# Two experts of a mixture-of-experts kernel are fixed in the first two whole units, and two shared units move in among the routed ones

## The reference

```python
def moe_ffn(h, router_w, router_bias, w_gu, w_down, shared_gu, shared_down):
    scores = jax.nn.sigmoid(jnp.dot(h, router_w, ...))
    _, idx = lax.top_k(scores + router_bias, TOP_K)          # TOP_K = 6 of 64 experts
    gates = jnp.take_along_axis(scores, idx, axis=-1)
    gates = gates / jnp.sum(gates, axis=-1, keepdims=True) * ROUTED_SCALE
    ...                                                      # no capacity limit, no dropped tokens
        y = swiglu(h_pad[src_b], w_gu[e], w_down[e])         # 1024 -> 2x384 -> 1024
        return y * gate_b[:, None]
    ...
    return routed + swiglu(h, shared_gu, shared_down)
```

## Time and profile before

| | us |
|---|---|
| median of 3 runs | 3029.93 (3028.95 to 3030.8) |
| the profiled execution, device time | 3032.81 |
| its span | 3030.9 |
| PE busy | 2432.6 (80%) |
| DVE / ACT / POOL busy | 800.4 / 425.1 / 316.4 |
| DMA moved | 776.00 MB, of which HBM read 770.98 MB |
| mean granted PE clock | 0.904 of full speed |

### The profile page before, as it was taken

The page is one execution under the profiler, slowest core; times in us unless marked ns, Lnnn a source line. Parts: engine busy times, 40 slices in busy tenths (PEclk is TensorE's granted clock), DMA queues, the critical chain, the costliest instruction groups (busy, mean ns, idle before and its releaser), DMA issues. The chain is left out here.

```text
span 3030.9 us, 36674 instructions
## 1 busy us (share of the span) xinstructions
PE 2432.6 (80%) x15133; PEld 1334.9 (44%) x15133; DVE 800.4 (26%) x1601; ACT 425.1 (14%) x854; POOL 316.4 (10%) x374
## 2 busy tenths in 40 slices
PE   5978869999899888988870797929877888888882
PEld 2447625555444444444430356816543434444331
DVE  2214564324211111111015413574421111111112
ACT  1022323310000000000000203215100000000000
POOL 0015200000011111110100004300001111101000
PEclk8989978799999999999995898959989999999996
DMA  7010266333899999999956110001489999999992
GB/s 266 24 51 3 71 224 224 128 123 124 327 426 424 416 400 402 390 402 406 398 213 256 47 46 2 3 9 67 183 347 428 421 419 421 413 413 416 410 393 108
DMA packets 122428, 776.00 MB, mean 256 GB/s; under 512 B 34648, under 2 KB 45032, under 8 KB 65808
## 3 DMA queue, kind: packets, MB, share of 16 engines
q1 hardware_dynamic: 99216, 735.75, 60.1%
q0 software_dynamic: 23040, 37.82, 3.3%
HBM read 770.98 MB, written 44.44 MB: 269 GB/s over the span
## 5 line engine op out<-in xcount | busy, mean ns | idle before, releaser
L1330 PE MATMUL banks<-arena,htreg 128*64 128x384 f32 (+1 forms) x4288 | 905.5, 515 | 129.3 <-DMA arena<-in_exp_w_gu 119.5
L1330 PEld LDWEIGHTS banks<-arena,htreg 128*64 128x64 f32 (+1 forms) x4288 | 448.0, 155 | 594.9 <-issue 366.8
L1350 PE MATMUL banks<-arena,modreg 128*64 128x512 f32 (+1 forms) x1608 | 439.9, 607 | 74.2 <-DMA arena<-in_exp_w_down 32.5
L1941 DVE TENSOR_TENSOR modreg<-modreg,banks 128x384 f32<-128x384 f32 x80 | 44.3, 554 | 967.2 <-ACT modreg L1564 967.2
L1350 PEld LDWEIGHTS banks<-arena,modreg 128*64 128x64 f32 (+1 forms) x1608 | 165.4, 150 | 294.9 <-issue 294.9
L2244 POOL DMA_INDIRECT y_d<-modreg,lst x74 | 73.6, 994 | 1362.8 <-DVE modreg L2081 1346.5
L953 PE MATMUL banks<-arena,htreg 128*128 128x428 f32 x512 | 184.2, 522 | 0.0
L1564 ACT ACTIVATE modreg<-banks 128x384 f32<-128x384 f32 x80 | 39.2, 490 | 998.0 <-PE banks L1330 998.0
L2081 DVE COPY modreg<-banks 128x512 f32<-128x512 f32 x74 | 51.2, 692 | 437.0 <-PE banks L1350 437.0
L953 PEld LDWEIGHTS banks<-arena,htreg 128*128 128x128 f32 x512 | 97.3, 190 | 86.9 <-issue 86.9
L1576 ACT ACTIVATE modreg<-banks 128x512 f32<-128x512 f32 x74 | 44.2, 597 | 440.0 <-PE banks L1350 440.0
(11 more groups left out here) (377 smaller groups left out, 2298.0 us busy)
## 6 DMA issues: line engine op xcount, KB each, us to landing
arena<-in_exp_w_gu SPq DMA_DIRECT2D x256, 1536.0 KB
arena<-in_exp_w_down SPq DMA_DIRECT2D x128, 1536.0 KB
modreg<-in_w_mod SPq DMA_DIRECT2D x40, 1024.0 KB, 5.0
arena<-y_d SPq DMA_DIRECT2D x6, 3072.0 KB, 17.6
arena<-in_w_in SPq DMA_DIRECT2D x8, 1712.0 KB, 10.8
modreg<-mod_d SPq DMA_DIRECT2D x20, 512.0 KB, 6.3
arena<-in_w_out SPq DMA_DIRECT2D x2, 4096.0 KB, 13.6
arena<-in_w_mod SPq DMA_DIRECT2D x6, 1024.0 KB, 9.3
```

Of the source, the lines that this page charges most:

```text
L1330: last = mm(ps[2 + half][rows, 0:DE], src[:, k, rows], up4[q][:, i, DE * half:DE * (half + 1)], start=(k == 0), stop=(k == KD - 1))
L1350: last = mm(ps[4 + half][rows, :], actT[:, k, rows], dn3[q][:, k, 512 * half:512 * half + 512], start=(k == 0), stop=(k == KE - 1))
```

## The change

Experts 0 and 1 get sort keys above all others, and so ranks 0 and 1, whatever their numbers of rows. SP loads their weights by constant index before it waits for the sort. The order of units becomes: two shared ones, then whole unit 0, the third shared, whole unit 1, the fourth shared (layer 1 has only two shared ones), then the rest, with whole units somewhat denser and the last four or five paired ones alone at the end. A chunk goes to the slot that comes free first. The shared units behind the first two get their transposed input in the way of a routed unit. On PE both list steps stand before `unit_down(1)`; on DVE the lists come before `unit_times(1)`, and the addresses of the general lists and `maxcnt` come behind the first `unit_copied`. `WHOLE`, `UNITS`, `cap` and the branch on `maxcnt` stay.

```diff
 WHOLE = (16, 4)
+GIVEN = 2
...
+        EARLY = 2
...
-            order = []
+            order = [whole.pop(0) for _ in range(GIVEN)]
+            early = len(paired) - 4
             for i in range(len(paired)):
                 order.append(paired[i])
-                while whole and (len(order) - i) * len(paired) <= (i + 1) * WHOLE[l]:
+                while whole and (len(order) - i - 1) * early < (i + 1) * WHOLE[l]:
                     order.append(whole.pop(0))
             return order + whole
...
+        def with_shared(l):
+
+            routed = work(l)
+            order = [(None, (i,)) for i in range(EARLY)]
+            for i in range(EARLY, NOUT[l]):
+                order += [routed.pop(0), (None, (i,))]
+            return order + routed
...
+        freed = lambda l, c: (c[0] or LAST_SHARED[l], PARTS.index(c[1]))
+
+        def ring(l):
+
+            slot_of, held = {}, {}
+            for i, c in enumerate(CHUNKS[l]):
+                q = i if i < SLOTS else min(held, key=lambda q: freed(l, held[q]))
+                slot_of[c], held[q] = q, c
+            return slot_of
...
                 sp.wait_ge(lists_cleared.sem, lists_cleared.at(l, 1))
-                sp.wait_ge(sorted_ready.sem, sorted_ready.at(l, 1))
...
+                    if r0_sorted(n):
+                        sp.wait_ge(sorted_ready.sem, sorted_ready.at(l, 1))
+                    experts = [r if r < GIVEN else sp.value_load(eid[0:1, r:r + 1], min_val=0, max_val=NE - 1) for r in ranks]
...
-                unit_up(1)
-                lists_by_expert()
+                unit_up(1, between=lists_by_expert if n_t == 2 else None)
+                if n_t > 2:
+                    lists_by_expert()
+                lists_by_unit()
                 unit_down(1)
-                lists_by_unit()
-                for n in range(2, NSH[l]):
-                    unit_up(n)
-                    unit_down(n)
-                unit_transposed(NSH[l])
-                for n in range(NSH[l], NW[l]):
+                unit_transposed(EARLY)
+                for n in range(EARLY, NW[l]):
                     unit_up(n)
                     if n + 1 < NW[l]:
                         unit_transposed(n + 1)
                     unit_down(n)
...
                 link(stt(key, cnt, float(NE), K("experts"), ALU.mult, ALU.subtract))
+                link(ts(key[:, 0:GIVEN], K("experts")[:, 0:GIVEN], -1.0, float(NO_CODE), ALU.mult, ALU.add))
...
-                unit_times(1)
                 dve.wait_ge(slot_hot_used.sem, slot_hot_used.at(l, TOPK * n_t))
                 dve.tensor_copy(listT, ps[1][lo64, 0:P]).then_inc(listT_ready.sem, 1)
-                shared_out(1)
...
+                unit_times(1)
+                shared_out(1)
...
+                unit_copied(EARLY)
+                overflow_addresses()
+                for n in range(EARLY, NW[l]):
...
-                pool.wait_ge(gu_psum.sem, gu_psum.at(l, NSH[l]))
+                pool.wait_ge(gu_psum.sem, gu_psum.at(l, EARLY))
```

More of the change, by code:

```diff
@@ L802, in load_expert, with one_of @@
                                  ).then_inc(X["w"][b].sem, 16)
+                def one_of(e):
+                    return slice(e, e + 1) if isinstance(e, int) else bass.ds(e, 1)
                 def load_chunk(c, experts):
@@ L826, in _ @@
                             if loaded >= SLOTS:
-                                m, was, _ = CHUNKS[l][loaded - SLOTS]
-                                m = max(m, NSH[l] - 1)
-                                sp.wait_ge(free_by[was].sem, free_by[was].at(l, m + 1))
+                                q = SLOT_OF[l][n, part, j]
+                                was = in_slot(l, q)[SEQ_OF[l][n, part, j] - 1]
+                                by = free_by[was[1]]
+                                sp.wait_ge(by.sem, by.at(l, freed(l, was)[0] + 1))
                             if loaded == SLOTS - 1:
@@ L1305, in unit_transposed @@
                 def unit_transposed(n):
[L1306 to L1309, removed]
+                    q = n - EARLY
+                    if is_shared(l, n):
+                        src = h[:, OUT_TILES[l][WORK[l][n][1][0]], :].rearrange("p (k d) -> p k d", k=KD)
+                    else:
+                        r = ROUTED_AT[l].index(n)
+                        pe.wait_ge(gathered[r % 2].sem, gathered[r % 2].at(l, r // 2 + 1))
+                        src = slots[r % 2].rearrange("p (d k) -> p k d", k=KD)
+                    if q:
+                        pe.wait_ge(slotT.sem, slotT.at(l, q))
                     for k in range(KD):
-                        last = pe.transpose(ps[k // 4][:, tok(k % 4)], slots[r % 2].rearrange("p (d k) -> p k d", k=KD)[:, k, :], ident)
+                        last = pe.transpose(ps[k // 4][:, tok(k % 4)], src[:, k, :], ident)
                     last.then_inc(slotT_psum.sem, 1)
                 def unit_up(n, between=None):
-                    if n >= NSH[l]:
-                        pe.wait_ge(slotT.sem, slotT.at(l, n - NSH[l] + 1))
-                        src = hgT[(n - NSH[l]) % 2]
+                    if n >= EARLY:
+                        pe.wait_ge(slotT.sem, slotT.at(l, n - EARLY + 1))
+                        src = hgT[(n - EARLY) % 2]
                     else:
@@ L2032, in _ @@
                          ALU.mult, ALU.mult))
[L2033 to L2049, removed]
+                def overflow_addresses():
+                    link(ts(base, rank, float(U_), float(HALF * U_ - U_ + W_), ALU.is_ge, ALU.mult))
+                    link(tt(base, base, rank, ALU.add))
+                    link(tt(cnt, cnt, cap, ALU.subtract))
+                    link(red(cntmax[:, 0:1], cnt, AX, ALU.max))
+                    link(ts(cntmax[:, 1:2], cntmax[:, 0:1], float(P), None, ALU.add))
+                    link(dve.tensor_copy(maxcnt[0:1, 0:1], cntmax[0:1, 1:2]))
+                    link(stt(adr[:, nt_, :], pos[:, nt_, :], float(U_), bc(base, 1, n_t), ALU.mult, ALU.add))
+                    link(stt(adr2[:, nt_, :], pos[:, nt_, :], float(NE), bc(K("experts"), 1, n_t), ALU.mult, ALU.add))
+                    link(stt(adr2[:, nt_, :], adr2[:, nt_, :], float(LIST1), adr[:, nt_, :], ALU.add, ALU.subtract))
+                    link(tt(adr2[:, nt_, :], adr2[:, nt_, :], over[:, nt_, :], ALU.mult))
+                    link(tt(adr[:, nt_, :], adr[:, nt_, :], adr2[:, nt_, :], ALU.add))
+                    for i in range(n_t):
+                        link(tt(ohp, onehot[:, i], bc(adr[:, i, :], 1, TOPK), ALU.mult))
+                        link(red(posk[:, i, 0:TOPK], ohp, AX, ALU.add))
+                    dve.tensor_copy(addr[:, nt_, 0:TOPK], posk[:, nt_, 0:TOPK]).then_inc(addr_ready.sem, 1)
@@ L2066, in unit_copied @@
                 def unit_copied(n):
[L2067 to L2073, removed]
+                    q = n - EARLY
+                    dve.wait_ge(slotT_psum.sem, slotT_psum.at(l, q + 1))
+                    dve.tensor_copy(hgT[q % 2][:, 0:4, :], ps[0][:].rearrange("p (k n) -> p k n", k=4))
+                    dve.tensor_copy(hgT[q % 2][:, 4:8, :], ps[1][:].rearrange("p (k n) -> p k n", k=4)).then_inc(slotT.sem, 1)
+                unit_copied(EARLY)
+                overflow_addresses()
+                for n in range(EARLY, NW[l]):
                     unit_times(n)
```

57 lines of the change are left out of this document (31 added, 26 removed).

## The result

| | before | after |
|---|---|---|
| median us | 3029.44 (3025.36 to 3030.8) | 12095.69 (12059.91 to 12145.55) |
| ratio | | 3.9937, 95% interval 3.9819 to 4.0055 |
| span of the profiled execution | 3030.9 | 12065.1 |
| mean granted PE clock | 0.904 | 0.808 |

The change makes the kernel four times as long. The forecast was 12,450 us, with 11,190 to 14,260 as its range. The four runs of the changed kernel lie 86 us apart, so a kernel with the loop that ran once is read to some tens of microseconds.

What follows compares the result with a forecast made beforehand. Both layers were taken as bound by streaming expert weights, PE close behind in layer 0. The sum was 3032.8 - 33 + 9470 = 12,470, less 2.9 to the runs' median, 12,467, said as 12,450 us; range 11,190 to 14,260.

Steps and rivals of the forecast that it cites:

- The branch: After layer 0's units: a 65-row expert at rank 16 exceeds cap 64, so 256 loop steps run; none in layer 1.
- The step of the loop: Layer 0's loop: load and matmuls follow one another, 37.0 us a step (32 to 44), 9470 us for 256 steps.
- load, issue to first matmul: Start of each loop step: 4608 KB of weights, scaled from w_out's landing, take 15.3 us.
- gathered rows in place: Loop step, beside the load: copy, scatter, gather and transposes take 10.0 to 19.9 us, about 13, hidden behind the load.
- gate and up: Loop step's first matmuls on PE: 10.48 us plus 2.9 for the low clock, 13.4 us (10.5 to 16).
- down: Loop step's down projection on PE: 5.39 us, up to 7.09 when the clock fell.
- the branch back: End of each loop pass over four steps: possible instruction fetch of 2.8 us, 180 us in all, making the time 12,650.
- rival 3: The gather sets the loop step's front, landing at 12.7 us: step 41.6 us, time 13,650; chance 8 in 100.
- The rest of the change: Everything outside the loop: early weights, layer 1's start, both layer ends and the moved list chain together give -33 us.
- By then 14 or 15 chunks are requested, as many as before at 815.: Layer 0's start: four units end near 811 with weight requests level with before; gain 3 us.
- PE follows the last landing by one down and little more, 7 us instead of 25.: Layer ends: with pairs last, PE finishes sooner after the last weights; gain 18 us in each layer.
- layer 1's start: Layer 1: two whole units first draw too few weight chunks, partly offset by lists 5.4 us sooner; net loss of 6.

Runs made afterwards that it cites:

- one_round: Changed kernel with R = [1, 1], so the loop makes one round of 64 experts instead of four; 5300.8 us (one run).
- key_only: Kernel before plus only the line giving experts 0 and 1 ranks 0 and 1; 12,091 us (one run), with 256 loop loads.
- fixed_1_15: Changed kernel with experts 1 and 15, the fullest of layer 0, fixed instead of 0 and 1; no loop, 3029.2 us, ratio 0.9992 to before.
- before_pairs_last: Kernel before with whole units mixed a little denser, so four or more paired units stand last in each layer; 3017.8 us, ratio 0.9954.
- fixed_late: fixed_1_15 with SP's wait for the sort put back ahead of the first expert's load; ratio 0.9995.
- fixed_even: fixed_1_15 with the old mixing of the other whole units, so a whole one stands last in both layers; 3044.9 us, ratio 1.0044.

## Why the prediction was right, and where it was off

**The branch.** Right as told. One row of expert 37 was over, layer 0 took the loop for it, layer 1 did not. The argument used counts only; no busy time of before could have shown it.

**The step of the loop.** Forecast 37.0 us, measured 35.3, inside the 32 to 44 taken. By terms:

| term | forecast | in the step shown | mean of all steps |
|---|---|---|---|
| load, issue to first matmul | 15.3 | 14.1 | 14.4 (with the last row) |
| gathered rows in place | 13, hidden | 13.4, hidden by 0.7 | |
| gate and up | 13.4 | 12.0 | 12.5 |
| silu to copy | 2.4 | 2.4 | 2.4 |
| down | 5.4 | 5.4 | 6.0 |
| branch, semaphores | 0.5 | 0.2 | |

The means are worked out from the page's lines of L1296, L1306, L1314 and L1320 above, busy and idle time over 256; they add up to 35.4. Two terms were too large: the front by 1.4 us (15.3 + 0.5 against 14.4), since two transfers of 3072 and 1536 KB came faster than scaled from w_out, and gate and up by 0.9. The down projection was too small by 0.6, since I took its fast case. The step shown is a short one of 34.1 us. Of the 255 distances between two loads 168 are near 34.2 us and 87 near 37.5. In a long one (1633.35 to 1670.65) gate and up took 13.40 and down 7.11 at a mean granted clock of 0.73, against 12.04 and 5.41 at 0.80 in the step shown.

For the branch back the Trainium skill, page "Runtime: NRT & Kernel Launch", section "Instruction fetch mechanics", has a taken branch out of the prefetched pages wait for a fetch. No such wait shows here, so the estimate of 2.8 us for each pass over four steps is not borne out. The step shown is the last of its pass, and the next load follows its down by 0.17 us; the same gap, 0.17 to 0.19, stands at all 63 places behind a branch back and within the passes. The instruction queues of the page hold 125 and 47 packets before and after alike, so they record no fetch for the loop's 64 passes beyond those of the kernel before. And one_round finds no cost besides the steps.

That the loads are not overlapped was right, and so was rival 3's mechanism in part: it shows at once when the load is moved away, but with 2.2 to 6.5 us for the landing, not 12.7.

**The rest of the change.** Here the forecast said -33. The trace of the changed kernel says -9, of which -11 is layer 1, where key_only reads -10 in the old order; and fixed_1_15, the change without the loop, says -2 (-6 to +1). The loop is so large that none of this touches the total. Two steps failed.

*"By then 14 or 15 chunks are requested, as many as before at 815."* The changed kernel had requested 14, but the kernel before had requested 19. The DMA view of 675:816, before and then after, has:

```profile
DMA packets 3867, 27.85 MB, mean 198 GB/s; under 512 B 1059, under 2 KB 1059, under 8 KB 1873
...
arena<-in_exp_w_gu SPq DMA_DIRECT2D x14, 1536.0 KB
arena<-in_exp_w_down SPq DMA_DIRECT2D x5, 1536.0 KB
```

```profile
DMA packets 3884, 24.40 MB, mean 173 GB/s; under 512 B 1268, under 2 KB 1268, under 8 KB 2215
...
arena<-in_exp_w_gu SPq DMA_DIRECT2D x10, 1536.0 KB, 7.7
arena<-in_exp_w_down SPq DMA_DIRECT2D x4, 1536.0 KB, 7.4
```

The 3.45 MB between them are 8.3 us at the 414 GB/s of the window behind it. Such a count is good to some 3 us: before_pairs_last, whose first units are those of before, moved 29.15 MB by then. But the four kernels with two fixed units at the head moved 24.4 to 25.3, and those without 27.9 to 29.9. The weights of layer 0 end 9 us later than before, near 1560 + 0.20 x 20 = 1564.0 where it was 1554.6. I had sized this as a gain of 3. Three slots stay with the shared expert until the fourth shared unit, and the two whole units before it draw three chunks each where the first two routed units before, pairs, drew six. The early loads, which look like the point of the change, are not even part of the balance (fixed_late).

*"PE follows the last landing by one down and little more, 7 us instead of 25."* The windows and timelines of both ends of the changed kernel:

```profile
1560.00:1580.00 20.00, 15.02 (x77) 6.79 (x74) 0.56 (x1) 0.98 (x2) 0.00 (x0) 0.91 0.20 83
11980.00:12000.00 20.00, 16.70 (x95) 8.24 (x93) 2.53 (x4) 1.58 (x3) 0.97 (x1) 1.00 0.72 297
```

```profile
1566.30 5.38 PE L1366 MATMUL banks<-arena,htreg 128*64 128x384 f32 x32 [3.02 <-DMA arena<-in_exp_w_gu]
1572.85 0.62 PE L1377 MATMUL banks<-const,modreg 128*128 128x128 f32 x3 [1.17 <-DVE modreg L1978]
1574.26 7.07 PE L1386 MATMUL banks<-arena,modreg 128*64 128x512 f32 x24 [0.78 <-ACT modreg L1602]
...
11997.40 5.38 PE L1366 MATMUL banks<-arena,htreg 128*64 128x384 f32 x32 [2.44 <-DMA arena<-in_exp_w_gu]
```

PE's last wait for weights ends at 1566.30. Behind it come the second half of gate and up (5.38), 2.6 us of small steps and a down projection of 7.07, where the same 24 records took 5.37 at 1550.60; the granted clock is 0.83 in 1570:1580, after 1.00 in the ten before it, in which PE idled for 3.02 us. That makes 15.0 us and not 7: the second half of gate and up and the steps between were left out. PE ends at 1581.3, 17 us behind the mark 1564.0, and in layer 1 at 12012.4, 18 us behind 11994.4. (These marks, like mine in the prediction, take the DMA's busy time as one piece. In the trace its share thins out instead, from 0.44 at 1560 to 0.26 at 1570; so they serve for differences only.) So the term was 8 us a layer and not 18.

Together: layer 0 has -8.4 from the end (25.7 down to 17.3) and +9.4 from the later weights, +1 in all. The experiments' traces say the same: PE ends layer 0 at 1573.4 in before_pairs_last, 6.9 us sooner than before, at 1588.2 in fixed_even and at 1581.9 in fixed_1_15. In layer 1 the end has -7.1 (25.1 down to 18.0), with ten pairs behind the last whole unit there and not the four or five that the section on the change names. What layer 1's start cost or won isn't known: I had put it at a loss of 6, and the -3.2 left of the -11 lies within what two traces of the same order differ by. So layer 1's forecast of -12 beside a reading of -11 was luck.

before_pairs_last and fixed_even bear out the end, 14 to 16 us for both layers where I had 36. fixed_even has +13 us against the kernel before for the rest of the change, where I had +3.

## What to carry to other kernels

Where a schedule has fixed capacities and a slow path behind them, a change of who gets which place is first a question of counts: sort them, apply the new assignment and look at the branch, before any busy time is read. One row over was worth 9000 us, because the slow path does all of its work for any overflow. A test per step, which skips an expert without rows left, is what the record suggests; it was not tried. And an earlier transfer is worth nothing where the next one waits for a buffer: look at what the queue waits for behind it, and count the bytes moved by a fixed time.

## What the runs showed of the hardware beyond that

The totals of the page do not fit the packets. The packets of the indirect DMAs' queue are 37.82 MB before and 38.12 after: 73,728 packets more for 0.30 MB, so addresses out of bounds show as packets of 4 bytes. But the page of the changed kernel has

```profile
HBM read 2113.15 MB, written 178.66 MB: 190 GB/s over the span
```

against 770.98 and 44.44 before (in the prediction I had the reads up by 1208 only). The written part rises by 134.2 MB, which is 256 x 128 rows of 4 KB; the read part by 1342.2, which is the weights' 1208 and another 134. In one_round, with 64 steps, 78.00 MB are written, 33.6 more than before and again 64 x 128 x 4 KB. So the totals count every row of an indirect DMA in the loop, in bounds or not. In time this does not show: the gather beside nothing else lands in 2.2 us, which for 128 full rows would be 238 GB/s after no latency at all. Whether those totals come from real transfers or from the descriptors' sizes was not tried.
